# Two attention mixers: probabilities turned by a transposing DMA instead of TensorE, and the second product moved behind gated tiles and token mixing

## The reference

```python
def _hybrid_mixer(h, w_in, b_gate, ..., w_pa, w_pb, w_out):
    proj = h @ w_in
    u, va, q, k, v, qi, ki, wi, g_a, g_b = jnp.split(proj, SPLIT_POINTS, axis=-1)
    y_a = _gmlp_spatial(u, va, ...) @ w_pa          # token mixing
    ...                                             # rope on q, k, qi, ki
    y_b = _dsa_attention(q, k, v, qi, ki, wi) @ w_pb
    gates = jax.nn.sigmoid(jnp.concatenate([g_a, g_b], axis=-1) + b_gate)
    gate_a, gate_b = jnp.split(gates, 2, axis=-1)
    return (gate_a * y_a + gate_b * y_b) @ w_out
# _dsa_attention, 8 heads of 64: scores over the 64 keys chosen by an index score, then
        p = jax.nn.softmax(s, axis=-1).astype(v.dtype)
        return jnp.einsum('bhqk,bqkhd->bqhd', p, v_sel)
# _gmlp_spatial: v = layer_norm(gelu(v)); mixed = einsum('gts,bnsgc->bntgc', lower triangle of w_s, v) + b_s; u * mixed
```

## Time and profile before

| | |
|---|---|
| median of three runs | 1518.04 us (1518.04 to 1518.24) |
| profiled execution, its own time | 1518.14 us |
| its span | 1516.1 us |
| TensorE busy | 1507.6 us, 99% |
| VectorE, ScalarE, GpSimd busy | 642.5, 483.2 and 1027.6 us |
| granted TensorE clock | 0.999 of full |

### The profile page before, as it was taken

How to read it: one execution, slowest core, us unless ns; L and a number is a source line. 1 busy time by engine, 2 the same in 40 slices (tenths; PEclk the granted TensorE clock), 3 DMA queues, 4 the chain that set the end, 5 groups by cost and what they waited for, 6 DMA issues and landing times.

```text
span 1516.1 us, 32762 instructions
## 1 busy us (share of the span) xinstructions
PE 1507.6 (99%) x13912; PEld 1173.1 (77%) x13914; DVE 642.5 (42%) x1525; ACT 483.2 (32%) x1261; POOL 1027.6 (68%) x565
## 2 busy tenths in 40 slices
PE   9999999999999999999999999999999999999998
PEld 7666888998666866669889966669888889888885
DVE  4332386445332333315844533325454535464532
ACT  3221164413221133204541232213443313343322
POOL 6976667667767677775586667773858565648653
PEclk9999999999999999999999999999999999999999
DMA  9665555556655566565545465664455554546551
GB/s 390 225 209 203 183 187 176 169 180 217 210 200 197 193 235 210 195 200 194 178 169 188 174 237 194 203 214 156 161 196 194 184 195 155 178 154 236 170 192 56
DMA packets 42625, 293.96 MB, mean 194 GB/s; under 512 B 4720, under 2 KB 5232, under 8 KB 8688
## 3 DMA queue, kind: packets, MB, share of 16 engines
q1 hardware_dynamic: 41760, 290.83, 55.0%
q10 hardware_dynamic: 720, 1.04, 0.2%
HBM read 290.81 MB, written 1.05 MB: 193 GB/s over the span
## 4 chain that ended last, share of the span: by engine, by line
PE 96%; DVE 2%; ACT 1%; DMA 0%; issue 0%; ACTq 0%; DVEq 0%
PE ps L778 26%; PE ps L660 15%; PE ps L661 15%; PE ps L662 15%; PE ps L779 13%; PE ps L679 1%; PE ps L681 1%; PE ps L680 1%; PE ps L873 1%; PE ps L893 1%; ACT ps L1316 1%; PE ps L865 1%; PE ps L827 0%; PE ps L738 0%; PE ps L828 0%; PE ps L829 0%
## 5 line engine op out<-in xcount | busy, mean ns | idle before, releaser
L630 POOL TENSOR_TENSOR w_low<-ring 128x1024 f16<-128x1024 f32 (+1 forms) x544 | 1008.8, 1881 | 377.8 <-DMA ring<-in_w 377.5
L660 PE MATMUL ps<-hP,ring 128*128 128x256 f16 (+1 forms) x1936 | 468.7, 257 | 0.4 <-DVE hP L1656 0.4
L661 PE MATMUL ps<-hP,ring 128*128 128x256 f16 (+1 forms) x1936 | 468.6, 257 | 0.0
L662 PE MATMUL ps<-hP,w_low 128*128 128x256 f16 (+1 forms) x1936 | 468.5, 257 | 0.0
L778 PE MATMUL ps<-hP,ring 128*128 128x512 f16 x1280 | 416.2, 379 | 0.0
L779 PE MATMUL ps<-hP,w_low 128*128 128x256 f16 x1280 | 348.9, 273 | 0.0
L778 PEld LDWEIGHTS ps<-hP,ring 128*128 128x128 bf16 x1280 | 125.2, 98 | 150.6 <-issue 0.2
L660 PEld LDWEIGHTS ps<-hP,ring 128*128 128x128 bf16 x1936 | 190.1, 98 | 22.2 <-issue 5.1
L661 PEld LDWEIGHTS ps<-hP,ring 128*128 128x128 bf16 x1936 | 189.4, 98 | 15.4
L662 PEld LDWEIGHTS ps<-hP,w_low 128*128 128x128 f16 x1936 | 189.4, 98 | 15.4
L778 PE MATMUL ps<-work,ring 128*128 128x512 f16 x528 | 171.8, 379 | 0.0
(11 more groups left out here) (280 smaller groups left out, 1747.8 us busy)
## 6 DMA issues: line engine op xcount, KB each, us to landing
ring<-in_w SPq DMA_DIRECT2D x261, 1024.0 KB, 4.8
ring<-in_w SPq DMA_DIRECT2D x12, 512.0 KB, 3.6
con<-in_const SPq DMA_DIRECT2D x1, 2812.0 KB, 18.2
gm<-in_gm SPq DMA_DIRECT2D x2, 1024.0 KB, 17.5
ring<-in_w SPq DMA_DIRECT2D x2, 768.0 KB, 4.9
ring<-in_w SPq DMA_DIRECT2D x2, 560.0 KB, 4.9
ring<-in_w SPq DMA_DIRECT2D x2, 544.0 KB, 3.5
xT<-in_x SPq DMA_DIRECT2D x3, 256.0 KB, 4.4
```

The lines of the kernel that those rows point to most:

```text
L630: nc.gpsimd.tensor_tensor(w_low[:, c % SLOTS, a:b], ring[:, c % SLOTS, a:b], w_high[:, c % SLOTS, a:b], ALU.subtract).then_inc(split.by((c ...
L660: nc.tensor.matmul(bank, w_high[:, slot, a:a + m], rhs(k, 0), start=(k == 0), stop=False)
L661: nc.tensor.matmul(bank, w_high[:, slot, a:a + m], rhs(k, 1), start=False, stop=False)
L662: mm = nc.tensor.matmul(bank, w_low[:, slot, a:a + m], rhs(k, 0), start=False, stop=(k == kt - 1))
```

## The change

For both units of A0 and A1 the turning leaves TensorE. VectorE writes the probabilities as 16-bit high and low parts at once (`normal_parts` in place of `normalise` and `low_turned`), and one transposing DMA, issued from ScalarE's queue (`turn_by_dma` in place of `copy_turned`), turns all 24 blocks of 128x128 into `probsTP`. TensorE waits for its semaphore at `values`. The order of TensorE's work changes too: two more tiles stand between the first unit's probabilities and `values(0)`, and `values(1)` stands behind the token mixing and two gb tiles. ScalarE's and VectorE's programs follow.

```diff
+        probsP = work[:, 0:4 * PACK].bitcast(F16).rearrange("p (h s n) -> p h s n", h=4, s=2)
...
                 def mix(s, u, v_of, high, low):
 
                     pe.wait_ge(*v_split.at((s, v_of)))
-                    pe.wait_ge(*turned_low.at((s, u)))
+                    if (s, u) in by_dma:
+                        pe.wait_ge(probs_turned, 16 * in_turn[s, u])
+                    else:
+                        pe.wait_ge(*turned_low.at((s, u)))
...
                     gemm("v", 3), gemm("u", 0), gemm("u", 1), gemm("u", 2), gemm("u", 3), gemm("va", 0)
-                    turn(s, 0)
-                    gemm("va", 1), gemm("va", 2)
+                    gemm("va", 1), gemm("va", 2), gemm("va", 3), gemm("ga", 0)
                     values(0)
-                    gemm("va", 3)
+                    gemm("ga", 1)
                     pe.wait_ge(*y_low.at((s, 0)))
                     unit(1)
-                    for n in range(5):
-                        gemm("ga", n)
-                    turn(s, 1)
-                    gemm("ga", 5), gemm("ga", 6)
-                    values(1)
-                    gemm("ga", 7), gemm("gb", 0), gemm("gb", 1)
-                    pe.wait_ge(*y_low.at((s, 1)))
+                    gemm("ga", 2), gemm("ga", 3), gemm("ga", 4), gemm("ga", 5)
+                    gemm("ga", 6), gemm("ga", 7), gemm("gb", 0), gemm("gb", 1)
                     for t in range(TT):
                         pe.wait_ge(*v_normed.at((s, t)))
+                    pe.wait_ge(*probs_ready.at((s, 1)))
...
-                    for n in range(2, 8):
-                        gemm("gb", n)
+                    gemm("gb", 2), gemm("gb", 3)
+                    pe.wait_ge(*ya_low.at((s, 1)))
+                    values(1)
+                    gemm("gb", 4), gemm("gb", 5), gemm("gb", 6), gemm("gb", 7)
+                    pe.wait_ge(*y_low.at((s, 1)))
...
+                def turn_by_dma(s, u):
+
+                    act.wait_ge(*probs_ready.at((s, u)))
+                    act.dma_start_transpose(probsTP[:, :, :, :].rearrange("p h s (a q) -> p (h s a) q", q=P),
+                                            probsP[:, :, :, :].rearrange("p h s n -> p (h s n)")).then_inc(probs_turned, 16)
...
+                def normal_parts(s, u):
+
+                    dve.wait_ge(*exps_ready.at((s, u)))
+                    chain.link(nc.vector.reciprocal(sums, sums))
+                    for t, (a, b) in enumerate(HALVES):
+                        r = sums[:, t, :].rearrange("p (h o) -> p h o", o=1).to_broadcast([P, 4, b - a])
+                        ins = nc.vector.tensor_tensor(probsP[:, :, 0, a:b], ps[:, 4:8, a:b], r, ALU.mult)
+                    chain.link(ins)
+                    for h in range(4):
+                        for t, (a, b) in enumerate(HALVES):
+                            ins = nc.vector.scalar_tensor_tensor(probsP[:, h, 1, a:b], ps[:, 4 + h, a:b], sums[:, t, h:h + 1],
+                                                                 probsP[:, h, 0, a:b], ALU.mult, ALU.subtract)
+                    ins.then_inc(probs_ready.by((s, u)), 1)
```

More of the change, by code:

```diff
@@ L419, in build @@
         written = ctx.enter_context(nc.semaphore("written"))
+        probs_turned = ctx.enter_context(nc.semaphore("probs_turned"))
         def chunk_landed(c):
@@ L484, in build @@
         probs_ready = signal("probs_ready", units)
-        turned = signal("turned", units)
-        turned_copied = signal("turned_copied", units)
-        turned_low = signal("turned_low", units)
+        by_dma = [(s, u) for s in MIX_A for u in (0, 1)]
+        in_turn = {unit: i + 1 for i, unit in enumerate(by_dma)}
+        by_pe = [unit for unit in units if unit not in by_dma]
+        turned = signal("turned", by_pe)
+        turned_copied = signal("turned_copied", by_pe)
+        turned_low = signal("turned_low", by_pe)
         v_split = signal("v_split", [(s, u) for s in mixers for u in (("v",) if s in MIX_A else ("av", "cvg", "bv"))])
@@ L1398, in mixer_a @@
                     take("va", 0)
-                    copy_turned(s, 0)
-                    take("va", 1)
+                    turn_by_dma(s, 0)
+                    take("va", 1), take("va", 2), take("va", 3), take("ga", 0)
                     y_parts(0)
-                    take("va", 2), take("va", 3)
+                    take("ga", 1)
+                    take("ga", 2)
                     exps(s, 1, HD ** -0.5)
-                    for n in range(5):
-                        take("ga", n)
-                    copy_turned(s, 1)
                     act.wait_ge(*variance.at(s))
@@ L1409, in mixer_a @@
                                          ).then_inc(deviation.by(s), 1)
-                    take("ga", 5)
-                    y_parts(1)
+                    take("ga", 3), take("ga", 4), take("ga", 5)
+                    turn_by_dma(s, 1)
                     take("ga", 6), take("ga", 7), take("gb", 0), take("gb", 1)
@@ L1415, in mixer_a @@
                         nc.scalar.activation(yaP[:, g, 0, :], ps[:, 4 + g, 0:T], ACT.Copy).then_inc(ya_high.by((s, g)), 1)
-                    for n in range(2, 8):
-                        take("gb", n)
+                    take("gb", 2), take("gb", 3)
+                    y_parts(1)
+                    take("gb", 4), take("gb", 5), take("gb", 6), take("gb", 7)
                     for n in range(DK):
@@ L1897, in mixer_a @@
                     shifts_a(0)
-                    normalise(s, 0)
-                    low_turned(s, 0)
+                    normal_parts(s, 0)
                     y_parts(0)
@@ L1908, in mixer_a @@
                     ins.then_inc(variance.by(s), 1)
-                    normalise(s, 1)
-                    low_turned(s, 1)
+                    normal_parts(s, 1)
                     dve.wait_ge(*deviation.at(s))
@@ L1918, in mixer_a @@
                         nc.vector.tensor_tensor(v, v, gmlp("ln_b"), ALU.add).then_inc(v_normed.by((s, t)), 1)
-                        if t == 0:
-                            y_parts(1)
                     for g in range(4):
```

## The result

The changed kernel takes 1538.7 us (median of 4 runs, 1536.68 to 1539.86) against 1518.07 for the kernel before: 1.34% slower, ratio 1.0134, 95% interval 1.0122 to 1.0145. Forecast were 1513.3 us and a range that ended at 1522. The profiled execution took 1538.87 us, its span is 1536.8.

The account below looks back on a forecast made before the run. TensorE, busy 99% of the span, was taken as the bound. From 1518.14 us, 5.24 of transposes were subtracted with no stall, giving 1512.9, and 0.4 added for switches and the thin margin: 1513.3 us, range 1512.4 to 1522.

Parts of the forecast that it names:

- the issue time: First unit of A0: `probs_ready` rises and the DMA can be issued at about 251.03.
- the eight new instructions: VectorE's eight scalar_tensor_tensor after the multiplications: four pairs 2.56 us plus 0.10, hidden from TensorE.
- the norm of `va_tok` is in time but thinly: VectorE before token mixing: `v_normed` rises at U + 21.6, 0.6 us before TensorE comes; no stall.
- the second product is never late: `values(1)` behind token mixing: the second DMA has 16.0 us, so even 14.9 lands in time.
- the ring has room: The transposing DMA may delay the ring's loads; a load late by 5 us costs nothing.
- the first DMA alone decides: Of each mixer's two DMAs, only the first unit's, wanted at `values(0)`, can make TensorE stall.
- 8.9 us: First unit: time from DMA issue at 251.03 until TensorE stands at `values(0)` at 259.97.
- A plain-speed transfer that yields wholly to the load: First DMA: 4.2 us at plain load rate plus 3.7 for the ring's load, 7.9 us, no stall.
- The upper bound of 14.9: DMA landing from above: 192 small pieces per engine at 67 ns, 12.9 us, plus 2.0 for landing.
- rival C: First DMA late by small-piece price: 14.9 us, 6.0 us stall at `values(0)` per mixer, 1525.3 us; chance 0.14.
- rival A: The forecast: the first DMA lands within 8.9 us, no stall, 1512.6 to 1514.5 us; chance 0.52.
- rival D: The DMA's 24 blocks go one after another, 48 us (31.4 by the skill's price): 1655 or 1589 us; chance 0.06.

Follow-up runs that it names:

- x1_apart: The changed kernel plus one SyncE wait holding the ring's loads until the first unit's transposing DMA has landed, in both mixers: 1513.21 us, ratio 0.9966.
- x2_second_only: The changed kernel with the first unit turned by TensorE as before, only the second unit by DMA: 1515.70 us, ratio 0.9983.
- x5_second_phase: x1_apart with a ring load started together with the second unit's DMA in A0, and held until that DMA landed in A1: 1528.04 us in one run.
- x4_load_first: The changed kernel with ScalarE taking va(1) before issuing the first unit's DMA, so the ring's load starts just ahead of it: 1524.49 us, ratio 1.0040.

## Why the prediction was wrong

**Right:** what bounds the kernel (x1_apart and x2_second_only gain what TensorE sheds: 5.1 of 5.24 and 2.6 of 2.62 us); the issue time (251.29 against 251.03); the eight new instructions, 2.69 us against 2.66, as this row of VectorE after shows:

```profile
248.56 2.69 DVE L1835 SCALAR_TENSOR_TENSOR work<-ps,work 128x128 f16<-128x128 f32 x8
```

Right too: that the norm of `va_tok` is in time but thinly (it ends at 305.01 in A0, the token mixing starts at 305.12), that the second product is never late in the changed kernel, that the ring has room, and that the first DMA alone decides. The ring's load was issued at 252.26, 1.11 us ahead of the 253.37 of before, where I had moved it by 1.31. Had the DMA landed in 8.9 us, the forecast 1513.3 would have stood: x1_apart has 1513.21.

**The step that failed** is the price of the DMA: "A plain-speed transfer that yields wholly to the load lands after 4.2 + 3.7 = 7.9 us". Two things in it. Alone it takes 5.5 us, not 4.2; that would have been harmless. And I added the load's time to it, as if two transfers on the same engines could at worst follow one another; in A0 the DMA took 24.8 us instead of 7.9, in A1 13.7. Measured over all kernels, by what the ring did at the issue:

| ring's loads | us from issue to landing |
|---|---|
| none until it has landed (x1_apart two, x5_second_phase three) | 5.5 each |
| one issued 0.01 to 2.1 us ahead, the next 3.1 to 5.4 us behind | 9.2, 9.3, 9.4, 9.5, 9.6, 9.6, 10.2, 10.4, 10.8, 11.0, 11.3, 12.3 |
| one issued 1.0 us behind, or (x5_second_phase, 27.7) one with it and the next 3.1 us behind | 13.7, 18.1, 23.0, 24.8, 27.7 |

The upper bound of 14.9, too, was exceeded four times, once in the changed kernel, and rival C, the right one in place and sign, ended at 1525.3 with it. Its mechanism was not the right one: it priced a small packet at 67 ns, and in x1_apart, with no load behind it, the DMA's packets take 21 ns each (72.6% of 16 x 5.7 us for 3104, the last of the rows below). That it pointed the right way was luck. The idle time of the engines on both sides of the load, which spoke for rival A, is of no use once the load has run into the DMA. And no rival had the second price of a wait, the clock: 4.4 of the 20.7 us.

The Trainium skill's page "VectorE: DVE Perf Modes", section "The three transpose paths", has 1309 ns for one block by DMA. Alone, 24 blocks land in 5.5 us, 0.23 us a block: rival D's serial reading of it is refuted, and what made the DMA late is not a price per block.

The packets of the traces, by queue (q1 carries the ring's loads, q10 the transposing DMA; packets, MB, share of 16 engines), tell the bad case from the good one. The rows are: the changed kernel's first DMA from 251.2 to 255.04, when the first packet of the load behind it begins, and from there to 276.2; the second DMA from 296.7 to that moment, 301.82; the first of x4_load_first from 252 to 261.07, and the second of x5_second_phase from 277.8 to 284.17, chosen in the same way; x1_apart's first from 251.3 to 257. (The windows end a few hundredths of a microsecond early, so the rows count up to 20 packets less than the text below.)

```profile
q10 hardware_dynamic: 1681, 0.43, 67.9%
...
q1 hardware_dynamic: 278, 2.03, 66.8%
q10 hardware_dynamic: 1423, 0.36, 22.5%
...
q10 hardware_dynamic: 2932, 0.75, 67.8%
...
q10 hardware_dynamic: 3020, 0.77, 62.3%
...
q10 hardware_dynamic: 1546, 0.40, 30.8%
...
q10 hardware_dynamic: 3104, 0.79, 72.6%
```

A DMA has 3072 packets of 256 bytes and 32 small ones. In the twelve landings of the table's second row at least 95% of the 3072 had begun before the first packet of the next load, and in the five of its first row no load came. In the five bad ones 1564, 1687, 1695, 2290 and 2294 had begun, and they landed after 27.7, 24.8, 23.0, 18.1 and 13.7 us, in this order. Behind that moment both sides crawl: in the changed kernel's first DMA a transposing packet takes 54 ns on average (22.5% of 16 x 21.16 us for 1423) against 21, and a load's 0.81 us. This also tells x4_load_first from x5_second_phase in A0. In both the load issued with the DMA went first and undisturbed; the next came 5.36 us behind in the one, when nearly all was moved, and 3.12 in the other, when half was.

**What stays open** is the mechanism in the engines. That a load hurts when its packets run into the DMA's is read from 22 landings; no run was built to test it alone. Nor do the runs show why two transfers under way together slow each other down so far: whether each engine alternates between the two queues, or the sixteen wait for each other, was not measured. The same issue times gave 13.7 us in one kernel and 18.1 in another, with 2294 and 2290 packets begun, and this is not explained.

The best version here is x1_apart: the whole change and one more wait, 1513.21 us, 0.34% under the kernel before.

## What to carry to other kernels

A transfer that shares the engines with a stream of loads is not priced by adding times: measure it alone and beside the stream, with the loads at several distances ahead and behind, and if it gates a saturated engine, hold the stream for its few microseconds where the ring has slack. The gain of moving work off the bounding engine is small and certain, the wait that takes its place can be many times larger, and a wait of some microseconds on TensorE costs more in slow clock: here 1.3 to 1.6 us behind waits of 3.2 to 4.9 us, 2.8 behind one of 16.

## What the runs showed of the hardware

- A transposing DMA of 24 blocks of 128x128, 16 bits, SBUF to SBUF, lands 5.5 us after issue with no load issued until it has landed, five times out of five; beside 1024 KB loads it took 9.2 to 12.3 us where at least 95% of its packets had begun before the next load's first packet, and 13.7 to 27.7 us where 51 to 75% had.
- Its issue holds ScalarE's queue for 3.6 to 3.7 us with no load issued until it has landed, for 3.5 to 6.3 us beside loads, and 8.01 in the worst case (x5_second_phase, A0).
- After waits of 16.0, 4.9 and 4.5 us TensorE's next product took 2.13 us instead of 1.18, after one of 3.15 us 1.88. In A0 of the changed kernel the granted clock was 0.50 until 282, six microseconds after work had begun again at 276.25.
